# One merged operand for the forget gate's weights, stacks in 32-row transfers and five adaLN blocks loaded early, in a two-layer streaming encoder

## The reference

```python
mod = silu(c) @ w_ada + b_ada                       # shift, scale, gate, twice (adaLN)
h = rmsnorm(x, norm1_g) * (1 + sc1) + sh1
rq, rk, rv, rg, fq, fk, fv, ff, dq, dk, dv = split(h @ w_in)
logf = log_sigmoid(ff + b_forget)                   # ff: 6 columns, one per fox head
r_out = silu(rg) * group_norm(retention(rope(rq), rope(rk), rv, state))
f_out = softmax(fq @ fk.T / 8 + F_q - F_k, causal) @ fv         # F = cumsum(logf)
p1, p2 = softmax of the two halves of rope(dq), rope(dk), chunk-causal
d_out = head_rmsnorm((p1 - lam * p2) @ dv) * (1 - lam_init)
x = x + g1 * (concat(r_out, f_out, d_out) @ w_out)
h = rmsnorm(x, norm2_g) * (1 + sc2) + sh2
x = x + g2 * (square(relu(h @ w_up)) @ w_down)
```

## Time and profile before

| | us |
|---|---|
| time, median of 3 runs | 3327.64 |
| lowest and highest | 3326.74, 3330.47 |
| the profiled execution's own time | 3326.87 |
| its span | 3325.1 |
| PE busy | 3224.1 |
| DVE busy | 1696.0 |
| ACT busy | 984.5 |
| POOL busy | 957.8 |

### The profile page before, as it was taken

How to read it: one execution, slowest core, us unless ns; L and a number is a source line. 1 busy time by engine, 2 the same in 40 slices (tenths; PEclk the granted TensorE clock), 3 DMA queues, 4 the chain that set the end, 5 groups by cost and what they waited for, 6 DMA issues and landing times.

```text
span 3325.1 us, 50329 instructions
## 1 busy us (share of the span) xinstructions
PE 3224.1 (97%) x19286; PEld 2894.2 (87%) x19286; DVE 1696.0 (51%) x3073; ACT 984.5 (30%) x1770; POOL 957.8 (29%) x690
## 2 busy tenths in 40 slices
PE   6999999899999999999999999999999999999998
PEld 3988897566799999999988879966678999999997
DVE  4746273674495555555573544156546633333335
ACT  3132222574451111111232313147635311111112
POOL 1312332221232333333332214212213233333332
PEclk8999999999999999999999999999999999999999
DMA  5512476535112222222222114563321011111112
GB/s 213 180 47 95 156 238 218 125 91 139 33 59 85 85 76 76 88 82 82 83 64 73 35 50 176 190 172 76 76 66 45 27 51 44 44 45 50 44 44 72
DMA packets 135351, 307.07 MB, mean 92 GB/s; under 512 B 53789, under 2 KB 74341, under 8 KB 131729
## 3 DMA queue, kind: packets, MB, share of 16 engines
q1 hardware_dynamic: 93584, 224.39, 23.4%
q10 hardware_dynamic: 41600, 80.44, 6.9%
HBM read 240.14 MB, written 57.90 MB: 90 GB/s over the span
## 4 chain that ended last, share of the span: by engine, by line
PE 90%; DVE 4%; SPq 2%; ACT 1%; ACTq 1%; issue 1%; DMA 1%; DVEq 0%
PE ps L1387 22%; PE ps L1358 19%; PE ps L1299 9%; PE ps L1232 8%; PE ps L1022 6%; PE ps L1212 5%; PE ps L1078 4%; PE ps L1169 3%; PE ps L1276 3%; PE ps L1004 2%; PE ps L1046 1%; DVE tn L2053 1%; PE ps L1334 1%; DVE h_lo L2066 1%; DVE x L2238 1%; PE ps L1113 1%
## 5 line engine op out<-in xcount | busy, mean ns | idle before, releaser
L768 POOL CAST w_hi<-raw 128x1024 fp32r<-128x1024 f32 x212 | 229.5, 1082 | 1862.5 <-PEq L1393 447.3
L2238 DVE SCALAR_TENSOR_TENSOR x<-ps,mod,x 128x352 f32<-128x352 f32 (+2 forms) x768 | 353.6, 489 | 431.5 <-PE ps L1387 351.5
L1387 PE MATMUL ps<-act_hi,w_hi 128*128 128x352 f32 x1536 | 496.0, 323 | 0.0
L1387 PE MATMUL ps<-act_hi,w_lo 128*128 128x352 f32 x1536 | 492.6, 321 | 0.0
L1387 PE MATMUL ps<-act_lo,w_hi 128*128 128x352 f32 x1536 | 492.1, 320 | 0.0
L1358 PE MATMUL ps<-h_hi,w_hi 128*128 128x352 f32 x1344 | 433.5, 323 | 0.0
L1875 ACT ACTIVATE relu_b<-ps,consts 128x352 f32<-128x352 f32 x192 | 106.4, 554 | 1103.5 <-PE ps L1358 1084.3
L1358 PE MATMUL ps<-h_hi,w_lo 128*128 128x352 f32 x1344 | 430.8, 320 | 0.0
L1358 PE MATMUL ps<-h_lo,w_hi 128*128 128x352 f32 x1344 | 430.4, 320 | 0.0
L1299 PE MATMUL ps<-pT,vb 128*128 128x512 f32 (+5 forms) x1080 | 401.3, 461 | 0.0
L2302 DVE TENSOR_REDUCE pm<-ps 128x1 f32<-128x512 f32 (+4 forms) x468 | 251.2, 548 | 243.3 <-PE ps L1169 158.8
(11 more groups left out here) (223 smaller groups left out, 6112.3 us busy)
## 6 DMA issues: line engine op xcount, KB each, us to landing
raw<-in_w SPq DMA_DIRECT2D x212, 512.0 KB, 3.6
ada_next<-in_w_ada SPq DMA_DIRECT2D x48, 512.0 KB, 4.2
ada_w<-in_w_ada SPq DMA_DIRECT2D x24, 512.0 KB, 5.9
kb<-scr_k SPq DMA_DIRECT2D x36, 328.0 KB
kb<-scr_k SPq DMA_DIRECT2D x120, 82.0 KB
qb<-scr_q SPq DMA_DIRECT2D x36, 264.0 KB
ada_nat<-in_w_ada_first SPq DMA_DIRECT2D x8, 1024.0 KB, 20.5
qb<-scr_q SPq DMA_DIRECT2D x120, 66.0 KB
```

The source lines that it names most:

```text
L768: pool.tensor_copy(hi, raw[:, uc % 2, 0:width]).then_inc(pool_hi, 1)
L1387: last = mm(ps[:, i % 6, 0:GW], w[:, k * 256 + o * 128:k * 256 + o * 128 + 128], (act_lo if low else act_hi)[:, k * T + g * GW:k * T + (g ...
L2238: last = v.scalar_tensor_tensor(xs, ps[:, bank, a - g * GW:b - g * GW], gs, xs, ALU.mult, ALU.add)
```

## The change

It has three parts. (1) *Forget gate.* `wf_raw` is [128, 2, 24] and `wf` one operand [128, 208]: for block k, the 6 high columns stand at 56 (k // 4) + 6 (k % 4), the low ones 32 further on; the rest is zero or belongs to other blocks. A matmul takes 128 columns from the first high one on, so its output rows 0 to 5 are the high products and rows 32 to 37 the low ones. Two passes (`h_hi`, `h_lo`) replace three. All three groups run between L1046 and L1067, in banks 6, 7 and 5; DVE evicts both parts of each (6 small operations) ahead of the adds of L1067's tiles, and `forget` adds the low part to the high part. The sixth item of PROJ waits for those evictions. (2) *Stacks.* The 2 x 16 rows of a piece move in one transfer of 32 rows: 8 transfers per stack. (3) *adaLN.* Blocks 24, 25 and 26 are issued behind unit 32 in PROJ, and ATT issues blocks 27 to 31.

```diff
--- before.py
+++ after.py
@@ -36,6 +36,7 @@
 PHASES = 5
 RET, OUT0, PROJ, ATT, MLP = range(PHASES)
 PRIME = 3
+F_BANK = [6, 7, 5]
 
 
 def rows(t):
@@ -157,7 +158,7 @@
 
 
 X_AFTER = [10, 11, 12, 13]
-STACK_DMAS = {2: 14, 1: 9}
+STACK_DMAS = {2: 8, 1: 9}
 
 
 def stacked(u):
@@ -222,7 +223,7 @@
 
 
 ADA_BEHIND = ada_behind()
-ADA_AFTER = {11: range(8, 10), 12: (10,), 13: (11,), 14: range(12, 19)}
+ADA_AFTER = {11: range(8, 10), 12: (10,), 13: (11,), 14: range(12, 19), 16: range(19, 22)}
 ADA_ATT = [22 + u for u in range(10)]
 ADA_PARTS_AT = [3, 8]
 ADA_SPOTS = [[(1, i) for i in range(0, 24, 2)],
@@ -393,9 +394,9 @@
     states, e = at("states", [128, 19, HD], F32, e)
     decay, e = at("decay", [128, PAIRS, 2, 128], F32, e)
     decay_s, e = at("decay_s", [TS, PAIRS, 2, TS], F32, e)
-    wf_raw, e = at("wf_raw", [128, 80], F32, e)
-    wf_hi, e = at("wf_hi", [128, 80], F32R, e)
-    wf_lo, e = at("wf_lo", [128, 80], F32R, e)
+    wf_raw, e = at("wf_raw", [128, 2, 24], F32, e)
+    wf, e = at("wf", [128, 208], F32R, e)
+    wf_parts = wf[:, 0:112].rearrange("p (a c) -> p a c", a=2)
     crossed_r = [cross_a, cross_b, cross_a, cross_b, cross_a, cross_a]
     rot_of = [(q_rot if what == "q" else k_rot)[j] for what, j in ROPES]
 
@@ -600,19 +601,19 @@
                 sem = stk_in[u % 6]
                 if m == 2:
 
-                    def part(src, which, y):
-                        r = 64 * y + 16 * a
-                        return src[n, which, r:r + 16]
+                    def part(src, which):
+                        return src[n, which].rearrange("(y b r) t -> b y r t", y=2, b=4)[a]
 
                     k, q = kb[buffer_of(u)], qb_[buffer_of(u)]
-                    for y in range(2):
-                        r = 16 * y
-                        sp.dma_start(k[r:r + 16, :].bitcast(F32), part(scr_k, 0, y)).then_inc(sem, 16)
-                        sp.dma_start(k[32 + r:48 + r, :].bitcast(F32), part(scr_k, 1, y)).then_inc(sem, 16)
-                        sp.dma_start(k[64 + r:80 + r, :].bitcast(F32), part(scr_k, 0, y)).then_inc(sem, 16)
-                        sp.dma_start(q[r:r + 16, 0:T].bitcast(F32), part(scr_q, 0, y)).then_inc(sem, 16)
-                        sp.dma_start(q[32 + r:48 + r, 0:T].bitcast(F32), part(scr_q, 0, y)).then_inc(sem, 16)
-                        sp.dma_start(q[64 + r:80 + r, 0:T].bitcast(F32), part(scr_q, 1, y)).then_inc(sem, 16)
+                    def rows32(buf, r, w):
+                        return buf[r:r + 32, 0:w].bitcast(F32)
+
+                    sp.dma_start(rows32(k, 0, NKEY), part(scr_k, 0)).then_inc(sem, 16)
+                    sp.dma_start(rows32(k, 32, NKEY), part(scr_k, 1)).then_inc(sem, 16)
+                    sp.dma_start(rows32(k, 64, NKEY), part(scr_k, 0)).then_inc(sem, 16)
+                    sp.dma_start(rows32(q, 0, T), part(scr_q, 0)).then_inc(sem, 16)
+                    sp.dma_start(rows32(q, 32, T), part(scr_q, 0)).then_inc(sem, 16)
+                    sp.dma_start(rows32(q, 64, T), part(scr_q, 1)).then_inc(sem, 16)
                     sp.dma_start(k[96:106, :].bitcast(F32), scr_rows[0:10]).then_inc(sem, 16)
                     sp.dma_start(q[96:104, 0:T].bitcast(F32), scr_rows[10:18, 0:T]).then_inc(sem, 16)
                 else:
@@ -669,9 +670,9 @@
                         if w == DIFFS:
                             sp.wait_ge(f_rows, (li + 1) * 32)
                         stack_load(li, w)
-                    if li == 0 and u < 8:
-                        sp.wait_ge(ada_done, 2 * (19 + u) + 2)
-                        back_load(24 + u)
+                    if li == 0 and u < 5:
+                        sp.wait_ge(ada_done, 2 * (22 + u) + 2)
+                        back_load(27 + u)
                     if li == 0 and u in X_AFTER:
                         sp.wait_ge(st, li * SLOTS + (u + 1) * NP)
                         sp.wait_ge(ada_done, 2 * sum(ADA_BACK))
@@ -1055,7 +1056,7 @@
                 pe.wait_ge(out0_ps, li * 48 + 24)
                 pe.sem_inc(w_used, 1)
 
-                forget_sums(li, (0, 1))
+                forget_sums(li, (0, 1, 2))
                 for i in range(24):
                     g, b = divmod(i, KB)
                     if i == 0:
@@ -1107,12 +1108,12 @@
                     if g == 0:
                         pe.wait_ge(o_kept, (li + 1) * (3 * PAIRS))
                     elif g == 2:
-                        pe.wait_ge(f_kept, li * 3 + 1)
+                        pe.wait_ge(rt_rstd, (li + 1) * (3 * PAIRS))
                     for k in range(KB):
-                        for w, low in ((wf_hi, 0), (wf_lo, 0), (wf_hi, 1)):
-                            last = mm(ps[0:32, 6 + g % 2, 0:GW], w[:, 6 * k:6 * k + 32],
-                                      (h_lo if low else h_hi)[:, k * T + g * GW:k * T + (g + 1) * GW],
-                                      start=(k == 0 and w is wf_hi and not low), stop=(k == KB - 1 and low == 1))
+                        for first, h in ((True, h_hi), (False, h_lo)):
+                            c0 = 56 * (k // 4) + 6 * (k % 4)
+                            last = mm(ps[:, F_BANK[g], 0:GW], wf[:, c0:c0 + 128], h[:, k * T + g * GW:k * T + (g + 1) * GW],
+                                      start=(k == 0 and first), stop=(k == KB - 1), skip_group_check=True)
                     last.then_inc(f_ps, 1)
 
             def forget_turned(li):
@@ -1198,6 +1199,8 @@
                     y = item[0] - li * P_ITEMS
                     if y < 6:
                         pe.wait_ge(out0_kept, (li + 1) * 48)
+                        if y == 5:
+                            pe.wait_ge(f_kept, (li + 1) * 6)
                     else:
                         pe.wait_ge(p_kept, item[0] - (5 if y < P_FEW + 3 else 2))
                     return bank_of(y)
@@ -1242,7 +1245,6 @@
                                 ring(li, q, *RING[q][2:])
                     u[0] += 1
 
-                forget_sums(li, (2,))
                 for m in (2, 1):
                     values(m)
                     for i in range(6):
@@ -2214,8 +2216,9 @@
                         ada_block(ADA_RET.index(y))
                     if y == 17:
                         dve.wait_ge(f_loaded, (li + 1) * 16)
-                        link(v.tensor_copy(wf_hi[:], wf_raw[:]))
-                        v.tensor_tensor(wf_lo[:], wf_raw[:], wf_hi[:].bitcast(F32), ALU.subtract).then_inc(f_wsplit, 1)
+                        link(v.memset(wf[:].bitcast(F32), 0.0))
+                        link(v.tensor_copy(wf_parts[:, :, 0:24], wf_raw[:]))
+                        v.tensor_tensor(wf_parts[:, :, 32:56], wf_raw[:], wf_parts[:, :, 0:24].bitcast(F32), ALU.subtract).then_inc(f_wsplit, 1)
                 if li == 0:
                     dve.wait_ge(x_back, 16)
                 for i in range(24):
@@ -2241,6 +2244,11 @@
             def out_first(li):
 
                 begin(dve, li, OUT0)
+                for g in range(GROUPS):
+                    cols = slice(g * GW, (g + 1) * GW)
+                    dve.wait_ge(f_ps, li * 3 + g + 1)
+                    v.tensor_scalar(fz[:, cols], ps[0:6, F_BANK[g], 0:GW], bias_f[:, li:li + 1], None, ALU.add).then_inc(f_kept, 1)
+                    v.tensor_copy(fe[:, cols], ps[32:38, F_BANK[g], 0:GW]).then_inc(f_kept, 1)
                 dve.wait_ge(out0_kept, li * 48 + 24)
                 for i in range(24):
                     g, b = divmod(i, KB)
@@ -2267,11 +2275,8 @@
                 dve.wait_ge(f_in, (li + 1) * 32)
 
             def forget(li):
-                for g in range(GROUPS):
-                    dve.wait_ge(f_ps, li * 3 + g + 1)
-                    v.tensor_scalar(fz[:, g * GW:(g + 1) * GW], ps[0:6, 6 + g % 2, 0:GW], bias_f[:, li:li + 1], None,
-                                    ALU.add).then_inc(f_kept, 1)
-                dve.wait_ge(f_kept, li * 3 + 3)
+                dve.wait_ge(f_kept, li * 6 + 6)
+                link(v.tensor_tensor(fz[:], fz[:], fe[:], ALU.add))
                 v.scalar_tensor_tensor(fe[:], fz[:], -1.0, fz[:], ALU.mult, ALU.max).then_inc(f_z, 1)
                 dve.wait_ge(f_z, li + 1)
                 link(v.tensor_scalar(fz[:], fz[:], 0.0, None, ALU.min))
@@ -2586,7 +2591,7 @@
     order += [np.concatenate([up, down], 2).reshape(L, 8 * MLP_CHUNKS, 128, UNIT)]
     a["w"] = c(np.concatenate(order, 1).reshape(L * NU, 128, UNIT))
     wf = i["w_in"][:, :, 7 * 384:7 * 384 + 6].reshape(L, KB, 128, 6).transpose(0, 2, 1, 3).reshape(L, 128, 48)
-    a["w_forget"] = c(np.concatenate([wf, np.zeros((L, 128, 32), np.float32)], 2))
+    a["w_forget"] = c(wf.reshape(L, 128, 2, 24))
     a["b_ada"] = blocks(i["b_ada"])
     a["norm_g"] = c(np.stack([blocks(i["norm1_g"]), blocks(i["norm2_g"])], 2))
     a["final_g"] = c(i["final_g"].reshape(KB, 128).T)
```

## The result

The changed kernel takes 3506.48 us (median of 4 runs, 3504.34 to 3509.05) where the kernel before takes 3327.32 us: ratio 1.0537, 95% interval 1.0518 to 1.0555, so 179 us slower. The forecast was 3478 us, 3400 to 3620. The profiled execution has a span of 3502.5 us, 177.4 us more than before.

What follows compares the result with a forecast made beforehand. The prediction took PE, with 90% of the chain that ended last, to bound the kernel. Forget part +13, projections +33 and attention +105 us summed to +151 us on 3326.9: 3478 us, range 3400 to 3620.

Steps and rivals of the forecast that it cites:

- Two engines per transfer: Stack transfers: the new source's outer dimension of 2 gives each transfer two DMA engines, not 16; chance 0.88.
- The price of a stack: One stack on two engines: 909 thousand bytes take 17.1 us, 18 us with end packets and rows.
- Attention: Stacks 2 to 11 follow each other on two engines until stack 11 lands: +47 us layer 0, +58 layer 1, +105 together.
- The sign that PE would stop at L1169 for each stack: In attention, PE would stop at L1169 for each stack from 2 to 11, with turns some 18 us apart.
- Two bounds of the prediction: Upper bounds for slow rows: 32 us per stack at the 64-row transfers' rate, and +395 us in attention.
- The projections: Unit 32 queues behind stacks and values on two engines: PE 13.7 us late, 16.3 per layer with slow clock, +33 both.
- The forget part: Start of projections: L1212 4.2 and 3.0 us later, slow clock 2.6 us per layer; with small DVE operations +13 us.
- POOL's hidden split: Start of projections: POOL's second weight split ends about where the forget sums do, so it bounds L1212 without them.
- DVE's 1.8 us: Six evictions ahead of DVE's residual adds start these 1.8 us later, delaying L1067, POOL and the projections by as much.
- contention: DVE's forget chain beside POOL's splits lengthens both: 2.5 us taken, bounds 0 and 4; 3.7 us by the skill's rule.
- The stall at 600 us goes: -12.4 us: Layer 0 attention: preload removes PE's stall around block 24 and its slow clock, -12.4 us unless stacks set the pace.
- Sixteen engines: Rival: stack transfers spread like today's; +13 sums, -12.4 block 24, -5 component 2, -0.6 small waits: 3322 us; chance 0.12.

Runs made afterwards that it cites:

- first16: The changed kernel with 16-row stack transfers for components 0 and 1 only, 32-row ones kept for 2 to 11: 3457.02 us, ratio 1.0386.
- block24_first: The kernel before, with adaLN block 24's load issued in attention ahead of the stacks of components 5, 6 and 7: 3316.82 us, ratio 0.9975.
- ry_only: The kernel before with 32-row stack transfers in (row, half) order alone, no preload and no forget part: 3312.16 us, ratio 0.9953.
- best3: The changed kernel with (row, half) transfers, forget evictions behind all residual adds, and L1067's tiles ordered by weight units: 3309.28 us, ratio 0.9942 to the kernel before.
- after_ry: The changed kernel with its 32-row transfer sources in (row, half) instead of (half, row) order: 3324.91 us, ratio 0.9994 to the kernel before.

## Why the prediction was right, and where its terms were off

*Two engines per transfer.* Right, and shown from three sides: 12 small packets for six transfers at 52 GB/s, the same loss with 16-row transfers whose sources are 2 x 8 rows, and the loss gone with 32-row transfers whose sources are 16 x 2 rows. The rule of the Trainium skill (DMA: Bandwidth & Descriptors, Why a DMA increments its semaphore by 16 and not by 1), for which the trace of before had no row at 2 against 32, is borne out at 2, 4 and 16. In all these cases the number that divides both sides is also the smaller of the two or 16, so these runs do not show that it is the divisor that counts.

*The price of a stack.* Forecast 18 us. SP, held in its issues, begins two stacks in a row, with nothing else issued between them, 17.6 us apart (timeline of SP):

```profile
656.06 0.62 SPq L611 DMA_DIRECT2D kb<-scr_k  x1
...
673.68 0.61 SPq L611 DMA_DIRECT2D kb<-scr_k  x1
```

Attention: forecast +47 and +58 us, found +54.2 and +59.7. What is over in layer 0 I put down to the value loads (PE waits up to 10.5 us at L1301) without a run for it. The sign that PE would stop at L1169 for each stack came in part only: 9 such stops in 20 components. In others PE stops for the maxima instead (L1278, 16 stops, 28.6 us in all), which the sum did not have, and works slowly behind that. From the turn of component 5 to that of 6 in layer 0 it waits for no stack, 2.1 us for maxima and 0.8 for DVE, and its own work takes 17.35 us at a clock of 0.83, for 14.26 at full clock before (windows of the changed kernel and of before: us, busy of PE, PEld, DVE, ACT, POOL, clock, DMA share, GB/s):

```profile
691.56:711.74 20.18, 17.35 (x61) 11.21 (x62) 11.48 (x27) 11.01 (x21) 8.58 (x3) 0.83 0.37 119
```

```profile
640.93:655.22 14.29, 14.26 (x61) 9.32 (x62) 11.27 (x27) 10.18 (x19) 8.59 (x3) 1.00 0.39 94
```

From the turn of component 8 to that of 10, in either layer, PE does not wait at L1170 at all, but for values (10.5 and 9.0 us) and maxima (3.7 and 3.9). So the pace of the two engines held, but that stack 11's landing ends the attention loss, as the sum had it, is not shown, and part of the agreement with +105 us may be luck.

Two bounds of the prediction do not come out of its rows: 909 thousand bytes at 2/16 of 218 GB/s take 33.4 us, not 32, and 32 us per stack give +385 us by the terms of the sum, not +395; nothing else rests on them.

*The projections.* Forecast 16.3 us per layer, and 4.2 + 2.6 and 3.0 + 2.6 for the start, 45 us in both layers; found 31.9 + 31.7. Here a term was mis-sized, and this makes 19 of the 26 us between the forecast +151 and the +177 of the profile: I let values and unit 32 queue on the two engines' data (5 us for the values), while SP is held in its issues. Values took SP from 529.55 to 547.18 us, 17.6 us, where they took 3.6 before, and PE waited 24.8 us for 13.7. first16 gives that part as 49 us, for 33 forecast.

*The forget part.* Forecast L1212 at 327.9 us, +4.2 and +3.0 us, and a slow clock; found 327.94 us in the kernel with this part alone and 327.38 in the changed one, 6.0 and 5.1 us per layer with the clock, for 6.8 and 5.6; timed alone +16 us for +13. The steps on POOL's hidden split, on DVE's 1.8 us and on contention are each in the trace. Their sizes are not quite those of the forecast: in the changed kernel POOL starts 1.8 us later and takes 9.6 us for its two splits instead of 7.7, so 1.9 us more for the 2.5 taken and the 3.7 that the prediction worked out beside them; in the kernel with this part alone POOL starts 2.4 us later, and that two errors cancel there is luck. The clock was 0.65 from 327 to 332 us. By the rule of the Trainium skill (SBUF — State Buffer, Who interferes with whom) two such operations wait for each other where they overlap: DVE's L2279 began at 319.35 us inside POOL's L773 (to 320.18) and took 0.69 us more than its 1.25; POOL's L774 began inside L2279 (to 321.29) and took 1.01 us more than its 1.27. Each waited about for the end of the other, and the rows agree.

*The preload.* In the sum it stood inside the stacks' pace, and so it cost the forecast nothing; but its mechanism was wrong. The step "The stall at 600 us goes: -12.4 us" holds for the wait and not for the time: alone it is 0 us, as the three loads lengthen ACT's store in the projections and the rows of maxima are late behind them. I had looked for what is queued behind the loads on SP, and not for who else has data on the same engines. The wait's cause was SP's issue queue, as block24_first and ry_only show.

*Sixteen engines.* The rival's time, 3322 us, was nearly met (3324.91), by terms of which two were wrong: +16 for the forget part, -15 for the transfers (forecast -5), and nothing for the preload (forecast -12.4).

What stays open: what gives the 3 us of layer 1 in ry_only (PE's wait for component 2 is 0.8 us shorter there, 4.6 for 5.4); what makes attention cost 7 us more than forecast in layer 0; and which of best3's parts makes it 3 us faster than ry_only, if it is.

## What to carry to other kernels

When transfers are merged, write out the access pattern of both sides and look at the outermost dimension: a pattern of 2 x 16 rows is moved by two engines, and exchanging the two loops (with the same exchange in all operands of the contraction) brings sixteen back. In these traces the small packets of one transfer, counted, tell its engines. And before a load is moved to an earlier place, ask which is late, the issue or the data: a long queue of issues on one engine is shortened by fewer issues or by one load put ahead, without new traffic where the engines are full.

## What was not expected of the hardware

A backlog on few engines holds the issuing engine. SP's issues, 0.42 us for the most part and 4.05 us at most before (L638 at 700.32 us), took up to 13.03 us in the changed kernel (L639 at 2244.71 us), and up to 7.07 us for rows of constants; with sixteen engines for the same transfers (after_ry) no such issue took over 3.7 us. An issue of 32 rows takes 0.59 us for 0.42 of one of 16. And a loss of engines that PE's pace hides later on is still seen at the first landings: at four engines (108 GB/s; 909 thousand bytes of a stack in 8.4 us by that rate, for PE's 14.2 us) the kernel lost 55 us.
